# A small unit of the busiest expert in the routing wait, in place of an overflow block, in a one-core decoder step

## The reference, cut to what matters

```
h = rms_norm(x) * (1 + sc1) + sh1;  z = h @ w_in                   # three mixers, gates, w_branch
x = x + g1 * (mixed @ w_out)                                       # "dense part"
h2 = rms_norm(x) * (1 + sc2) + sh2
group = argmax(h2 @ w_router_g + b)                                # 4 groups of 8 experts
top-2 experts inside the group, weights softmax(top 2) * group probability
y[t] = sum over its 2 experts of w * (silu(h2 @ w1[e]) * (h2 @ w3[e])) @ w2[e]
x = x + g2 * y;  out = rms_norm(x)
```

## Time and profile before

| | us |
|---|---|
| median of 3 runs | 1599.32 (1599.06 to 1599.82) |
| the profiled execution, its own time | 1599.82 |
| its span | 1598.0 |
| the 1.82 us around it | launch and end |
| PE busy | 1556.4 (97%) |
| DVE busy | 1256.8 (79%) |
| ACT busy | 808.1 (51%) |
| POOL busy | 371.3 (23%) |

### The profile page before, as it was taken

The page is one execution under the profiler, slowest core; times in us unless marked ns, Lnnn a source line. Parts: engine busy times, 40 slices in busy tenths (PEclk is TensorE's granted clock), DMA queues, the critical chain, the costliest instruction groups (busy, mean ns, idle before and its releaser), DMA issues.

```text
span 1598.0 us, 23304 instructions
## 1 busy us (share of the span) xinstructions
PE 1556.4 (97%) x9097; PEld 1335.3 (84%) x9097; DVE 1256.8 (79%) x1699; ACT 808.1 (51%) x885; POOL 371.3 (23%) x274
## 2 busy tenths in 40 slices
PE   6999999999999999999999999999999999999994
PEld 3777788878889999999999997788888888888882
DVE  4668877756747988886655459999999999999996
ACT  4222232235333223323242357788878887888775
POOL 2311000000000000002000202355665455445441
PEclk9999999999999999999999999999999999999998
DMA  9966322425334323232422667999999999999976
GB/s 332 327 190 195 89 80 82 150 80 152 117 97 146 119 81 92 67 93 85 130 80 81 215 228 271 352 392 378 400 400 373 381 379 383 390 379 388 396 262 242
DMA packets 219025, 362.48 MB, mean 227 GB/s; under 512 B 19806, under 2 KB 168382, under 8 KB 193562
## 3 DMA queue, kind: packets, MB, share of 16 engines
q1 hardware_dynamic: 196476, 323.10, 56.6%
q0 software_dynamic: 21792, 35.72, 7.7%
q10 hardware_dynamic: 646, 2.15, 0.3%
HBM read 363.16 MB, written 32.34 MB: 247 GB/s over the span
## 4 chain that ended last, share of the span: by engine, by line
PE 89%; DVE 5%; DMA 3%; issue 1%; ACT 1%; DVEq 1%; POOL 0%; SPq 0%; POOLq 0%; ACTq 0%
PE z L2975 16%; PE z L2977 16%; PE z L2976 16%; PE z L923 7%; PE z L921 7%; PE z L922 7%; PE z L938 3%; PE z L940 3%; PE z L939 3%; PE q L2866 2%; PE q L910 2%; PE q L2885 1%; DVE wl L1312 1%; DVE conv L2395 1%; DMA ada_h<-in_w_ada_dram 1%
## 5 line engine op out<-in xcount | busy, mean ns | idle before, releaser
L1312 DVE TENSOR_TENSOR wl<-wr,whr 128x2048 fp32r<-128x2048 f32 x196 | 442.3, 2284 | 0.6 <-ACT whr L679 0.5
L2975 PE MATMUL z<-h_hi,w_hi 128*128 128x272 f32 (+1 forms) x1248 | 407.4, 326 | 1.1 <-DVE h_lo L2214 0.6
L2977 PE MATMUL z<-h_hi,w_lo 128*128 128x272 f32 (+1 forms) x1248 | 402.9, 323 | 0.0
L2976 PE MATMUL z<-h_lo,w_hi 128*128 128x272 f32 (+1 forms) x1248 | 401.8, 322 | 0.0
L679 ACT ACTIVATE whr<-wr 128x2048 fp32r<-128x2048 f32 x196 | 370.9, 1911 | 53.9 <-PE z L923 52.6
L2214 DVE TENSOR_TENSOR w_lo<-w_raw,w_hi 128x1024 fp32r<-128x1024 f32 (+1 forms) x168 | 179.5, 1069 | 125.7 <-ACT w_hi L1911 125.7
L2975 PEld LDWEIGHTS z<-h_hi,w_hi 128*128 128x128 f32 x1248 | 235.1, 188 | 26.8 <-issue 8.2
L2977 PEld LDWEIGHTS z<-h_hi,w_lo 128*128 128x128 f32 x1248 | 234.8, 188 | 16.8
L2976 PEld LDWEIGHTS z<-h_lo,w_hi 128*128 128x128 f32 x1248 | 235.3, 189 | 15.8 <-issue 0.2
L921 PE MATMUL z<-whr,xTh 128*128 128x512 f32 x528 | 208.8, 395 | 0.0
L923 PE MATMUL z<-wl,xTh 128*128 128x512 f32 x528 | 206.1, 390 | 0.0
(11 more groups left out here) (484 smaller groups left out, 2310.6 us busy)
## 6 DMA issues: line engine op xcount, KB each, us to landing
wr<-in_w_dram SPq DMA_DIRECT2D x198, 1024.0 KB, 7.4
w_raw<-in_w_in_dram SPq DMA_DIRECT2D x104, 512.0 KB, 3.8
ada<-in_w_ada_dram SPq DMA_DIRECT2D x6, 2048.0 KB, 13.6
w_raw<-in_w_branch_dram SPq DMA_DIRECT2D x48, 256.0 KB, 2.8
w_raw<-in_w_out_dram SPq DMA_DIRECT2D x16, 512.0 KB, 4.0
ada_h<-in_w_ada_dram SPq DMA_DIRECT2D x2, 2048.0 KB, 15.2
ada_u<-in_w_ada_dram SPq DMA_DIRECT2D x2, 2048.0 KB, 9.9
ada_m<-in_w_ada_dram SPq DMA_DIRECT2D x2, 2048.0 KB, 10.7
```

Source lines behind the costliest of these rows:

```text
L1312: return dve.tensor_tensor(out, a, b, op)
L2975: pe.matmul(out, w_hi[w][:, k, :], hi[:, k, t0:t1], start=(k == 0), stop=False)
L2976: pe.matmul(out, w_hi[w][:, k, :], lo[:, k, t0:t1], start=False, stop=False)
L2977: last = pe.matmul(out, w_lo[w][:, k, :], hi[:, k, t0:t1], start=False, stop=(k == kn - 1))
```

## The change

The block list is 32 blocks (NB = NE), and in front of them comes a unit, "block" -1, of six weight chunks. It takes up to 64 rows (XR) of the expert that is busiest among the first 512 tokens, and these rows are taken out of that expert's ranks. The unit's 4 up chunks and 2 down chunks run as plain float32 products, without ACT's and DVE's split, at the places where `keep_busy` stood. Each product has 64 stationary columns and comes in two halves, h = 0 and 1, that write PSUM partitions 0 to 63 and 64 to 127. The unit's expert and tokens are worked out by DVE at the start of group 1's output projection; SP reads the expert's number from `first_e` before it issues the unit's first chunk. The ranks' one-hots of group 0 move behind that. The unit's result is added to the rows in HBM by an accumulating transfer of its own, for which block 0's result waits. SP's wait for `m_xg[0]` and the overflow block with all that served it go; overflow that is left would now all be done by the loop at the end. The diff, cut to what matters:

```diff
-NB = NE + 1
+NB = NE
+NX = 6
+XR = 64
...
-        CHUNKS = [(0, "up", c) for c in range(4)]
+        CHUNKS = [(-1, "up", c) for c in range(4)] + [(-1, "down", 0), (-1, "down", 1)]
+        CHUNKS += [(0, "up", c) for c in range(4)]
...
-            sp.wait_ge(m_xg[0], 16)
-            for n in range(RN - 1, 10 * RN):
+            for n in range(RN - 1, NCH):
                 load(n, CHUNKS[n][0])
-            sp.wait_ge(xrow_ok, 1)
-            sp.wait_ge(tab_sc, 16 * 2 * NT)
-            e_more = sp.value_load(xrow[0:1, 1, 0:1], min_val=0, max_val=NE - 1)
-            b_more = sp.value_load(xrow[0:1, 2, 0:1], min_val=1, max_val=NBLK - 1)
-            sp.dma_start(xcol[:], table[bass.ds(b_more * (P * NE), P * NE), :].rearrange(
-                "(r e) o -> r e o", e=NE)[:, bass.ds(e_more, 1), :].rearrange("r e o -> r (e o)"),
-                allow_slow_non_contiguous=True).then_inc(o_i, 16)
-            for n in range(10 * RN, NCH):
-                load(n, CHUNKS[n][0] if CHUNKS[n][0] < NE else e_more)
...
+            pool.wait_ge(oh_ok, 2)
+            for h in range(2):
+                pool.dma_start(first_g[64 * h:64 * h + 64, :], mod_dram[0:1, 512 * h:512 * h + 512].to_broadcast([64, 512])
+                               ).then_inc(first_g_in[0], 16)
             pool.wait_ge(tok_ok, 1)
             gather(0)
             gather(1)
...
+                    pool.wait_ge(first_tok_ok[0], first_tok_ok[1] + 2)
+                    pool.indirect_dma_start(x1_dram.rearrange("t (h d) -> (t h) d", h=2),
+                                            bass.IndirectOffsetOnAxis(ap=first_to[:, 0:1], axis=0), first_y[:], None,
+                                            bounds_check=2 * TOK - 1, oob_is_err=False, compute_op=ALU.add
+                                            ).then_inc(first_sc[0], 16)
...
-        def keep_busy(pe, n):
-            for _ in range(n):
-                pe.matmul(z[0][:, 0, 0:P], ident[:], ident[:], start=True, stop=True)
+        def first_up(pe, c, i0, i1):
+            if i0 == 0:
+                pe.wait_ge(m_ld[c], 16)
+            for i in range(i0, i1):
+                k = KF * (c % 2) + i
+                for h in range(2):
+                    last = pe.matmul(z[0][64 * h:64 * h + 64, c // 2, 0:FF // 2], first_T[:, k, :],
+                                     wr[c][:, i * FF + FF // 2 * h:i * FF + FF // 2 * h + FF // 2],
+                                     start=(k == 0), stop=(k == KD - 1))
+            if i1 == KF:
+                last.then_inc(m_c, 1)
+        def first_down(pe, c):
+            pe.wait_ge(m_ld[4 + c], 16)
+            for i in range(2):
+                k = 2 * c + i
+                for h in range(2):
+                    last = pe.matmul(z[1][64 * h:64 * h + 64, 0, :], first_gT[:, k % 2, 64 * (k // 2):64 * (k // 2) + 64],
+                                     wr[4 + c][:, i * D + 512 * h:i * D + 512 * h + 512], start=(k == 0), stop=(k == KF - 1))
+            last.then_inc(m_c, 1)
         def moe_tensor(pe):
-            keep_busy(pe, 4)
+            pe.wait_ge(first_copied[0], first_copied[1] + 1)
+            first_up(pe, 0, 0, KF)
+            first_up(pe, 1, 0, 1)
...
-            keep_busy(pe, 7)
+            first_up(pe, 1, 1, KF)
+            first_up(pe, 2, 0, 3)
...
-            keep_busy(pe, 21)
+            first_up(pe, 2, 3, KF)
+            first_up(pe, 3, 0, KF)
+            q_wait_read(pe, "pos")
+            pe.wait_ge(first_g2[0], first_g2[1] + 1)
+            for j in range(2):
+                last = pe.transpose(q[1][:, 0, j * P:(j + 1) * P], first_gs[:, j * P:(j + 1) * P], ident[:])
+            last.then_inc(first_pe[0], 1)
+            pe.wait_ge(parts_ok[0], parts_ok[1] + 1)
+            for t in range(PT):
+                for k in range(2):
+                    last = pe.matmul(z[1][:, 1, 256:259], first_ones[:, k, t, :], wpart[:, :, k, t],
+                                     start=(t + k == 0), stop=(t == PT - 1 and k == 1))
+            last.then_inc(first_wp[0], 1)
+            pe.wait_ge(first_copied[0], first_copied[1] + 2)
+            first_down(pe, 0)
             q_wait_read(pe, "tb")
...
-            keep_busy(pe, 4)
+            first_down(pe, 1)
...
+            high(NX + 3)
+            act.wait_ge(m_c, 2)
+            act.activation(first_hs[:], z[0][:, 0, 0:FF // 2], ACT.Silu).then_inc(first_sg[0], 1)
+            high(NX + 4)
+            act.wait_ge(first_pe[0], first_pe[1] + 2)
+            act.activation(first_gT[:], q[1][:, 0, 0:2 * P].rearrange("p (j t) -> p j t", t=P), ACT.Copy).then_inc(first_copied[0], 1)
             dense_done(act)
-            high(HN - 1)
+            high(NX + 5)
...
+            act.wait_ge(first_g_in[0], first_g_in[1] + 32)
+            act.wait_ge(first_w_ok[0], first_w_ok[1] + 1)
+            act.activation(first_g[:], first_g[:], ACT.Copy, scale=first_w[:, 0:1]).then_inc(first_fac[0], 1)
...
+            tt(wpart[:, 2], far[:], wpart[:, 1], ALU.subtract).then_inc(parts_ok[0], 1)
+            dve.tensor_copy(first_to[:], first_tok[:, 1:2])
+            dve.wait_ge(first_sg[0], first_sg[1] + 1)
+            dve.wait_ge(m_c, 4)
+            tt(first_gs[:], first_hs[:], z[0][:, 1, 0:FF // 2], ALU.mult).then_inc(first_g2[0], 1)
+            low(NX)
+            dve.wait_ge(first_wp[0], first_wp[1] + 1)
+            dve.tensor_reduce(first_w[:], z[1][:, 1, 256:259], axis=AX.X, op=ALU.add).then_inc(first_w_ok[0], 1)
...
+            low(NX + 1)
+            dve.wait_ge(m_c, NX)
+            dve.wait_ge(first_fac[0], first_fac[1] + 1)
+            tt(first_y[:], z[1][:, 0, :], first_g[:], ALU.mult).then_inc(first_tok_ok[0], 1)
...
+                    if b == 1:
+                        dve.wait_ge(first_sc[0], first_sc[1] + 16)
...
+                        if j == WS - 1:
+                            sp.wait_ge(first_ok[0], first_ok[1] + 1)
+                            e_first = sp.value_load(first_e[0:1, 0:1], min_val=0, max_val=NE - 1)
                         for n in {WS - 1: (0, 1), WS: (2,), WS + 1: (3,), WS + 2: (4,)}[j]:
-                            chunk_load(sp, n, CHUNKS[n][0])
-            moe_sync(sp)
+                            chunk_load(sp, n, e_first)
...
+            pool.wait_ge(first_tok_ok[0], first_tok_ok[1] + 1)
+            pool.wait_ge(h2_out, 16 * PT)
+            pool.indirect_dma_start(first_x[:], None, h2_dram[0:HALF, :], bass.IndirectOffsetOnAxis(ap=first_tok[0:XR, 0:1], axis=0),
+                                    bounds_check=HALF - 1, oob_is_err=False).then_inc(first_in[0], 16)
             moe_gpsimd(pool)
...
+            act.wait_ge(first_pe[0], first_pe[1] + 1)
+            act.activation(first_T[:], q[1][:, 0, :].rearrange("p (k t) -> p k t", t=XR), ACT.Copy).then_inc(first_copied[0], 1)
             for n in range(2):
-                weight_high(act, n)
+                weight_high(act, NX + n)
...
+                        dve.tensor_copy(em[:, 2 * PT, :], q[s][:, 0, PT * NE:(PT + 1) * NE])
                         own_ranks(dve, s, 0, PT, (em[:, 0:PT], em[:, PT:2 * PT])).then_inc(q_free[s], 1)
-                        rank_ones(dve, ohr0, 0, PT)
-                        token_ones(dve, ohv0, 0, PT).then_inc(ohr_ok, 1)
...
+                def first_expert():
+                    counts = em[:, 2 * PT, :]
+                    dve.max(m8f[:], counts)
+                    for h in range(2):
+                        dve.tensor_scalar(io64[:, :, h, :], io32[:].unsqueeze(1).to_broadcast([P, 2, NE]), 1.0 + NE * h, None, ALU.add)
+                    dve.drain()
+                    dve.max_index(i8f[:], m8f[:], counts)
+                    dve.tensor_scalar(less[:], m8f[:, 0:1], float(XR), -1.0, ALU.min, ALU.mult)
+                    dve.tensor_copy(codes0[:, :, 0], vlo[:, 0:1].to_broadcast([P, PT]))
+                    dve.drain()
+                    dve.tensor_copy(first_f[:], i8f[:, 0:1])
+                    dve.tensor_copy(first_e[:], i8f[:, 0:1]).then_inc(first_ok[0], 1)
+                    dve.tensor_scalar(share[:], less[:], 1.0 / P, None, ALU.mult)
+                    dve.tensor_copy(codes0[:, :, 1], vhi[:, 0, 0:PT])
+                    dve.drain()
+                    dve.tensor_scalar(ohf[:], io32[:], first_f[:, 0:1], None, ALU.is_equal)
+                    dve.tensor_scalar(isf[:], ef[:, 0:PT, :], first_f[:, 0:1], None, ALU.is_equal)
+                    dve.drain()
+                    dve.tensor_scalar(taken[:], ohf[:], share[:, 0:1], None, ALU.mult)
+                    mine = isf[:].rearrange("p t k -> p k t")
+                    dve.scalar_tensor_tensor(rkf[:], rk[:, :, 0:PT], 1.0, mine, ALU.add, ALU.mult)
+                    dve.drain()
+                    dve.scalar_tensor_tensor(rk[:, :, 0:PT], mine, less[:, 0:1], rk[:, :, 0:PT], ALU.mult, ALU.add)
+                def first_slots():
+                    for k in range(2):
```

(62 more changed lines are left out.)

129 lines of the change are left out of this document (65 added, 64 removed).

## The result

The change makes the kernel slower. Its median is 1604.38 us (8 runs, 1601.55 to 1606.44), that of the kernel before on the same chip 1599.44 (8 runs, 1599.05 to 1600.50): a ratio of 1.0028, 95% interval 1.0018 to 1.0037. Forecast were 1592.2 us and a range of 1586 to 1600. The profiled execution took 1601.55 us (span 1599.7), the fastest of the eight; the kernel before had 1599.82 (span 1598.0). So the trace explains +1.7 us of span, and the median is another 2.8 above it.

A forecast was written before the change was run, and what follows sets the result against it. The prediction took PE to bound the expert blocks, at 17.75 us per block. Its terms, -17.75 + 1.1 + 0.6 + 1.1 + 3.2 + 0.8 + 3.3 = -7.65 us, took 1599.82 to 1592.2 us, range 1586 to 1600.

The forecast's parts named there:

- The bound: Expert blocks: PE, with no idle time, sets the time at 17.75 us per block; the weight stream waits for PE.
- the block: Expert blocks: one block fewer, 32 instead of 33, takes off 17.75 us.
- the unit's products: Routing wait: halves run beside each other; four up chunks and one down take 10.8 us, at no cost.
- rival (c): Routing wait: the unit's six chunks hold PE and delay block 0; 1616 us, or 1605 in between; chance 0.15.
- Its sign, products past 988: Profile after: PE's new products running past 988 us would show that rival (c) holds.
- Rival (d): End of kernel: a row routed otherwise sends one block through the extra loop; over 50 us, 1650; chance 0.02.
- SP's wait for the expert's number: Output projection: holds chunks 0 and 1 and three `w_out` slices; 2 us of slack, no cost, 3 us if issue stretches.
- Working out the unit's rows: Output projection: PE stands 0.8 us for DVE's one-hots and 8 small products cost 0.3; +1.1 us (0.3 to 3).
- The stream no longer held: Routing wait: chunks from 12 on run before and beside gather 0, which lands in 6.5 us; +3.2 us (1.4 to 7.4).
- From the transposes to the first product: Start of block 0: the last down chunk, 2.0 us, stands where `keep_busy` took 0.91; +0.8 us (0 to 2.5).
- The unit's scatter: DVE's first `result`: waits for the accumulating transfer, taken to land in 8 us; +3.3 us (0 to 6.1).
- POOL's two broadcasts: Routing wait: two issues of 0.60 us each on POOL ahead of gather 0; +1.1 us (0.8 to 1.4).

The follow-up runs named there:

- e3: The changed kernel with POOL issuing the unit's accumulating transfer before its wait for the gate indices; 1599.49 us.
- e1: The changed kernel with DVE reading the product `first` at the end of j = 0, not behind the next weight split; 1598.70 us.
- e6: The e4 kernel with DVE working out table rows and gate indices at the start of block 1's turn; 1584.78 us, ratio 0.9907.
- e8: The e6 kernel with SP's wait for block 0's gathered rows removed again, so the stream is released; 1591.79 us, ratio 0.9953.
- e4: The changed kernel with the edits of e1, e2 and e3 together; 1590.08 us, ratio 0.9939.
- e2: The changed kernel with SP's wait for block 0's gathered rows put back, so the stream is held; 1597.97 us.
- e7: The changed kernel with 18 throw-away products on PE behind the unit's first down chunk, in its wait for gather 0; 1604.00 us.

## Why the prediction was wrong

The bound, the block and the unit's products were right: 17.75 us came off, the period stayed, the unit's four up chunks and first down chunk (9.3 us of PE work, 10.8 forecast) found room in the wait, and rival (c), in which they hold PE, did not happen. Its sign, products past 988, was there (988.85), but only because all of it came later; PE then had 4.66 us to wait. Rival (d), the extra loop, did not happen either: the tail adds 0.7 us and not 50. SP's wait for the expert's number cost nothing in the profile of after, but by luck: the slice of `w_out`, issued at 910.52, landed 8.6 us later, just where ACT begins its split (919.13), so of the 2 us of slack there was none. In e3 the slice's transfer lies on the chain. The forecast failed in the terms between.

**The step "Working out the unit's rows" is where the most was lost**: forecast 1.1 us, with 3 as the upper end, measured 6.0 at the last output tile. I costed the new product `first` at 0.3 us and its DVE readers not at all. I asked when its operands would be ready, and never when its PSUM buffer would be free again. That depended on where in DVE's order the reader stood: behind a split that waits for ACT. e1 shows it: reader moved, wait gone, 5.7 us.

**"The stream no longer held"** had the right mechanism and too small a size: +3.2 us forecast (1.4 to 7.4), +5.5 measured, inside its bounds. I took a value near the low rows (3.30, 4.7, 5.96), although the backlog of chunks was the very thing that these rows did not have; the stream's median of 10.7 was the nearer row. Its other half was left out: what a released stream gains. e6 against e8 says it gains nothing, since chunk 12 is block 1's first chunk and not needed for another block.

**"From the transposes to the first product"**, +0.8 forecast and +2.1 measured, failed with it. The sum left PE busy up to the landing, by its own numbers only just; when PE stood 4.66 us, the clock fell to 0.71 behind it. It stayed under the upper end, 2.5.

**"The unit's scatter"**: +3.3 forecast (0 to 6.1), +5.2 measured up to T. Again the right wait, and a landing of 9.85 us where I took 8. In nine traces it took between 9.0 and 11.6, though it moves half the bytes of a block's (10.8): half the bytes did not mean less time.

**"POOL's two broadcasts"**: they cost the 1.14 us that was forecast, but the term came out at -1.1, below its lower end (0.8), because the h2 rows landed 3.9 us sooner than forecast; then the token numbers released the gather, 1.94 us after POOL was ready. That the rows set this wait no longer held, and this error was in the forecast's favour: luck, 2.2 us of it.

So five of six terms came out above their value, and the one with the missed wait beyond its upper end: in the profile 8.6 us more than forecast. The prediction added up the high ends to about +5 and the low ends to -13.5; its terms give +3.65 and -14.85. It set the high ends aside as unlikely, and it took the chance for slower from (c) and (d) alone. But the terms are not independent. The gather and the scatter both land beside the same full stream, and each of the three stands of PE (3.60, 4.66 and 5.08 us) is followed by a low clock.

**Open.** The median is 2.8 us above the profiled execution, and eight runs spread over 4.9 us. e4, e6 and e8 spread over 1.0, 1.2 and 1.0, in four runs each, and e8 still has its wait for gather 0, so that wait alone does not make the spread. It goes with the clock: of the eight executions of after the two fastest have a mean granted clock of 0.990 and 0.991 and the other six 0.986 to 0.989, and in e2 the three slowest (1599.75 to 1600.72) have 0.987, the other seven 0.990 or 0.991. I have one profile of each kernel and can't say at which point the others lost it. For the same reason the single gains (5.7, 6.4, 4.9) are differences of medians, and in the profiles they are 2.6, 4.8 and 0.6.

## What to carry to other kernels

A unit that fills a wait is cheap in the engine that waited and dear in everything around it: for each new product ask which buffer it holds, who reads it, and what stands before that reader. A block removed pays up to its whole period, as far as the waits that its replacement makes are gone: here 14.9 of 17.75 us came out once three pieces of code were moved and the hold was back (1599.72 to 1584.78), and without that 4.9 us were lost. A hold on a stream is not slack: before lifting it, ask what the stream needs soon (here nothing) and what small transfer it would then stand beside.

## What the runs showed of the hardware

- A gather of 128 rows of 4 KB landed in 3.3 to 3.7 us with the stream held, 5.6 beside one chunk of 1 MB that was issued 0.8 us before it and some 3 where the chunk was 3.6 us ahead, and 8.8 to 9.8 beside a stream that may send all it has.
- PE stood 3.60, 4.66 and 5.08 us in the changed kernel, and in the window in which it came back the granted clock was 0.75, 0.71 and 0.50, in the one behind 0.82, 0.86 and 0.82. Throw-away products in the second of these waits kept it at 1.00 (e7). In e8, with a stand of 5.01 us and 0.55 and 0.60 behind it, PE took 6.5 us from its transposes to block 0's first product, and 4.3 in e6, which has no such stand.
- The unit's accumulating transfer of 64 rows of 4 KB, given as 128 half rows, took 9.0 to 11.6 us to land, as long as a block's of 128 rows.
